# Retention and mLSTM heads issued in turn on TensorE with four branch-gate projections between them, in other buffers and another order on VectorE and ScalarE

## What is computed

```python
hx = modulate(rms_norm(x, norm1_gain[layer]), sh1, sc1)
feats_x, post_x = mixer_inputs(hx, w_in[layer], mlstm_gate_bias[layer], rope)
ret_x, ml_x, _, _ = bidirectional_scans(feats_x, log_gamma[layer], st_f, st_b)
x = x + g1 * mixer_output(ret_x, ml_x, *post_x, w_ret_up[layer], w_ml_up[layer], w_out[layer])
x = x + g2 * swiglu(modulate(rms_norm(x, norm2_gain[layer]), sh2, sc2), w_ffn_in[layer], w_ffn_out[layer])
...
def mixer_output(ret, ml, rg, mo, bg_ret, bg_ml, w_ret_up, w_ml_up, w_out):
    y_ret = from_heads(head_norm(ret)).astype(dtype) * jax.nn.silu(rg)
    y_ml = from_heads(head_norm(jax.nn.sigmoid(to_heads(mo, ML_HEADS)) * ml)).astype(dtype)
    merged = jax.nn.sigmoid(bg_ret) * (y_ret @ w_ret_up) + jax.nn.sigmoid(bg_ml) * (y_ml @ w_ml_up)
    return merged @ w_out
```

## Time and profile before

| | |
|---|---|
| median of 3 runs | 2170.63 us (2169.23 to 2170.95) |
| the profiled execution | 2171.23 us, of it the span from first to last instruction 2169.5 us |
| TensorE busy in the span | 1827.0 us (84%) |
| VectorE, ScalarE, GpSimd busy | 669.6, 325.3, 70.5 us |
| bytes read from HBM | 579.83 MB, 268 GB/s over the span |
| mean granted TensorE clock | 0.915 of full |
| chain that ended last | PE 60%, DMA 32%, DVE 4%, ACT 2% |

### The profile page before, as it was taken

How to read it: one execution, slowest core, us unless ns; L and a number is a source line. 1 busy time by engine, 2 the same in 40 slices (tenths; PEclk the granted TensorE clock), 3 DMA queues, 4 the chain that set the end, 5 groups by cost and what they waited for, 6 DMA issues and landing times.

```text
span 2169.5 us, 23007 instructions
## 1 busy us (share of the span) xinstructions
PE 1827.0 (84%) x9806; PEld 1118.0 (52%) x9806; DVE 669.6 (31%) x1390; ACT 325.3 (15%) x668; POOL 70.5 (3%) x82
## 2 busy tenths in 40 slices
PE   7999789999998999998998888888999755565555
PEld 4557578788886456656443222224577522222222
DVE  3874265187832024523111011113232200000002
ACT  4101230100101123311110000003232100000001
POOL 0001210000000000000000000000040000000000
PEclk8999999999998975797999999999999888878888
DMA  9488225567536110021999999995322599999996
GB/s 410 205 367 330 78 83 228 195 271 286 223 121 255 70 54 1 1 78 64 429 428 427 428 428 428 427 426 217 121 112 78 218 428 427 427 427 427 427 427 260
DMA packets 42150, 582.37 MB, mean 268 GB/s; under 512 B 4672, under 2 KB 4928, under 8 KB 6080
## 3 DMA queue, kind: packets, MB, share of 16 engines
q1 hardware_dynamic: 42048, 580.90, 64.7%
HBM read 579.83 MB, written 1.05 MB: 268 GB/s over the span
## 4 chain that ended last, share of the span: by engine, by line
PE 60%; DMA 32%; DVE 4%; ACT 2%; issue 1%; POOL 1%; SPq 0%; DVEq 0%; ACTq 0%; POOLq 0%
PE banks L622 41%; DMA ring<-in_experts_dram 31%; PE banks L1145 6%; PE banks L1166 3%; PE banks L920 3%; PE banks L531 2%; PE banks L967 1%; PE banks L607 1%; DMA ring<-in_weights_dram 1%; DVE ring L1783 1%; DVE banks L1817 1%; PE banks L582 0%; PE banks L594 0%; PE banks L1233 0%; DVE hT L1855 0%
## 5 line engine op out<-in xcount | busy, mean ns | idle before, releaser
L1145 PE MATMUL banks<-ring,arena 128*32 128x256 f32 (+1 forms) x3072 | 398.6, 524 | 175.2 <-DMA ring<-in_experts_dram 173.4
L622 PE MATMUL banks<-hT,ring 128*128 128x256 f32 (+2 forms) x1776 | 407.4, 391 | 14.1 <-ACT hT L1401 12.2
L622 PEld LDWEIGHTS banks<-hT,ring 128*128 128x128 f32 (+1 forms) x1776 | 336.4, 190 | 84.6 <-issue 40.5
L1145 PEld LDWEIGHTS banks<-ring,arena 128*32 128x32 f32 (+1 forms) x3072 | 145.7, 134 | 426.0 <-DMA ring<-in_experts_dram 243.5
L1783 DVE SCALAR_TENSOR_TENSOR ring<-ring,sil_c 128x512 f32<-128x512 f32 x336 | 242.6, 750 | 7.9
L1166 PE MATMUL banks<-ring,arena 128*32 128x256 f32 (+1 forms) x1536 | 185.8, 486 | 67.0 <-DMA ring<-in_experts_dram 50.9
L2361 DVE TENSOR_TENSOR arena<-arena,banks 128x512 f32<-128x512 f32 (+1 forms) x32 | 17.7, 554 | 543.1 <-PE banks L1145 543.1
L622 PE MATMUL banks<-ring,hT 128*128 128x512 f32 (+1 forms) x448 | 176.1, 553 | 3.3 <-DVE arena L1992 3.3
L622 PE MATMUL banks<-arena,ring 128*128 128x256 f32 (+2 forms) x656 | 170.8, 421 | 2.7 <-POOL arena L2492 1.6
L622 PE MATMUL banks<-arena 128*128 128x64 f32 (+3 forms) x736 | 142.3, 354 | 23.8 <-POOL arena L2486 16.0
L1166 PEld LDWEIGHTS banks<-ring,arena 128*32 128x32 f32 (+1 forms) x1536 | 69.6, 126 | 166.7 <-issue 78.8
(11 more groups left out here) (279 smaller groups left out, 1135.9 us busy)
## 6 DMA issues: line engine op xcount, KB each, us to landing
ring<-in_experts_dram SPq DMA_DIRECT2D x192, 2048.0 KB, 30.5
ring<-in_weights_dram SPq DMA_DIRECT2D x73, 2048.0 KB, 11.5
ring<-in_weights_dram SPq DMA_DIRECT2D x8, 1408.0 KB, 7.3
ring<-in_weights_dram SPq DMA_DIRECT2D x2, 1152.0 KB, 26.5
cT<-in_ctx_dram SPq DMA_DIRECT2D x2, 1024.0 KB, 7.5
ring<-in_weights_dram SPq DMA_DIRECT2D x2, 1024.0 KB, 15.4
ring<-in_weights_dram SPq DMA_DIRECT2D x1, 1536.0 KB, 28.3
xT<-in_x_dram SPq DMA_DIRECT2D x1, 1024.0 KB, 7.1
```

Source lines behind the costliest of these rows:

```text
L622: ins = mm(dst, a, b, start=(i == 0), stop=(i == len(terms) - 1))
L1145: ins = mm(banks[M * q:M * q + M, which, 0:W], xc[:, 4 * half + k, :], w[:, k, W * q:W * q + W], start=(half == 0 and k == 0), stop=(half ...
```

## The change

Six things are changed:

- **TensorE.** The two head loops become one. For each h it issues gate projection h (`bg00`, `bg01`, `bg10`, `bg11`), both kinds of scores of head h+1, then both kinds of values of head h. The gates of b = 2 and 3 follow after the loop.
- **Buffers.** `p_ret` and `q_ret`, which overlapped `p_ml` and `q_ml` in the arena, move into the first half of slot `EARLY`, which holds `mod_acc[0]`. ScalarE and VectorE therefore wait once for `modT3`. `sig_r` moves to `hctx`, `yT` and `merged` move within the arena.
- **ScalarE.** The first four gate jobs are copied raw into `sig_r` between the heads; one Sigmoid over 2048 columns follows after the norms. It copies all four `yT` jobs.
- **VectorE.** The two head loops become one as well. `mod_sum` of c0 and c1 stays behind `y_normed`; c2 moves to just before the first `wo` residual and c3 to between the second and the third. Its two `yT` copies go away.
- **GpSimd.** The multiplications of the two kinds of heads alternate.
- **Order of the weights.** bg0 bg1 bg2 c0 bg3 c1 r_up c2 m_up c3, where it was bg0 c0 bg1 c1 bg2 c2 bg3 c3 r_up m_up.

The core of the diff:

```diff
-    for b in range(4):
-        w8(f"bg{b}", w_in, 4112 + 512 * b, 512)
-        w8(f"c{b}", m_w[1], 512 * b, 512)
+    for n in ("bg0", "bg1", "bg2", "c0", "bg3", "c1"):
...
     w8("r_up", w["w_ret_up"][0], 0, D)
+    w8("c2", m_w[1], 512 * 2, 512)
     w8("m_up", w["w_ml_up"][0], 0, D)
+    w8("c3", m_w[1], 512 * 3, 512)
...
-        p_ret = carve(G0 + 768, 2, 512)
-        q_ret = carve(G0 + 1792, 2, 2, N)
+        p_ret = ring[:, EARLY, 0:1024].rearrange("p (a n) -> p a n", a=2)
+        q_ret = ring[:, EARLY, 1024:2048].rearrange("p (a d n) -> p a d n", a=2, d=2)
...
-        yT = hctx
-        sig_r, sig_m = carve(0, KD, N), carve(2048, KD, N)
-        merged = carve(4096, KD, N)
+        yT = carve(4096, KD, N)
+        sig_r, sig_m = hctx, carve(0, KD, N)
+        merged = carve(6160, KD, N)
...
@@ TensorE @@
+            ret_scores(0)
+            ml_scores(0)
+            for h in range(HEADS):
+                branch_gate(h // 2, h % 2)
                 if h + 1 < HEADS:
+                    ret_scores(h + 1)
                     ml_scores(h + 1)
...
+                ret_values(h)
+                ml_values(h)
+            for b in (2, 3):
                 for a in range(2):
...
+                    branch_gate(b, a)
@@ ScalarE @@
+            def gate_copy(h):
+
+                job = f"bg{h // 2}{h % 2}"
+                eng.wait_ge(*jobs.is_filled(job))
+                A(flat(sig_r[:, 2 * h:2 * h + 2, :]), jobs.bank(job)[:, :], ACT.Copy).then_inc(*act.frees(job))
...
+            ret_decays(0)
+            eng.wait_ge(flag("mc_rep"), 1)
             ml_exps(0)
             for h in range(HEADS):
+                gate_copy(h)
+                if h + 1 < HEADS:
+                    ret_decays(h + 1)
+                    ml_exps(h + 1)
                 ml_abs(h)
...
+            A(flat(sig_r), flat(sig_r), ACT.Sigmoid).then_inc(*act.raises("sig_r"))
+            for b in (2, 3):
...
@@ VectorE @@
+            ret_weights(0)
             ml_weights(0)
             for h in range(HEADS):
+                ml_scored(h)
+                if h + 1 < HEADS:
+                    ret_weights(h + 1)
+                    ml_weights(h + 1)
+                ret_out(h)
                 ml_out(h)
...
-            for b in range(4):
-                mod_sum("c", b)
...
+            mod_sum("c", 0)
+            mod_sum("c", 1)
...
             for a in range(4):
+                if a in (0, 2):
+                    mod_sum("c", 2 + a // 2)
                 residual(f"wo{a}", xT, 2 * a, 0, 2, 0)
```

More of the change, by code:

```diff
@@ L749, in ret_scores, with ret_values @@
                                  for s in range(TC)]).then_inc(*jobs.fills(job))
-            eng.wait_ge(*jobs.is_drained("s_ret1"))
-            ret_scores(0)
-            for h in range(HEADS):
-                if h + 1 < HEADS:
-                    ret_scores(h + 1)
+            def ret_values(h):
                 eng.wait_ge(flag("ret_q"), 2 * h + 2)
@@ L766, in _, with branch_gate @@
                                  for c in range(TC)]).then_inc(*jobs.fills(job))
+            def branch_gate(b, a):
+                eng.wait_ge(*arrives(f"bg{b}"))
+                w = slot(f"bg{b}", 512)
+                job = f"bg{b}{a}"
+                if jobs.new(job) > 1:
+                    eng.wait_ge(*jobs.is_free(job))
+                o = jobs.bank(job)
+                project([(o[:, N * j:N * j + N],
+                                  [(w[:, k, P * (2 * a + j):P * (2 * a + j) + P], hlat[:, k, :])
+                                   for k in range(KD)]) for j in range(2)]).then_inc(*jobs.fills(job))
+                used(f"bg{b}", job)
+            eng.wait_ge(*jobs.is_drained("s_ret1"))
             eng.wait_ge(*jobs.is_drained("s_ml11"))
@@ L784, in ml_scores, with ml_values @@
                                  for s in range(TC)]).then_inc(*jobs.fills(job))
-            ml_scores(0)
-            for h in range(HEADS):
+            def ml_values(h):
                 eng.wait_ge(flag("ml_q"), 2 * h + 2)
@@ L826, in _ @@
             ups = [slot("r_up", D), slot("m_up", D)]
-            eng.wait_ge(*jobs.is_drained("yT01"))
-            eng.wait_ge(*jobs.is_drained("yT11"))
+            for m in range(2):
+                for a in range(2):
+                    eng.wait_ge(*jobs.is_drained(f"yT{m}{a}"))
             for n in range(KD):
@@ L1488, in _, with ret_decays @@
                 A(mo[:, c, :], o[:, :], ACT.Sigmoid).then_inc(*act.frees(f"x_mo{c}"))
-            for h in range(HEADS):
+            def ret_decays(h):
                 if h >= 2:
                     eng.wait_ge(*jobs.is_filled(f"ro{h - 2}"))
+                elif h == 0:
+                    eng.wait_ge(*jobs.is_filled("modT3"))
                 for d in range(2):
@@ L1541, in _ @@
                     o = jobs.bank(f"bg{b}{a}")
-                    dst = (sig_r, sig_m)[b // 2][:, 4 * (b % 2) + 2 * a:4 * (b % 2) + 2 * a + 2, :]
-                    A(flat(dst), o[:, :], ACT.Sigmoid).then_inc(*act.frees(f"bg{b}{a}"))
-            for a in range(2):
-                eng.wait_ge(*jobs.is_filled(f"yT0{a}"))
-                o = jobs.bank(f"yT0{a}")
-                A(flat(yT[:, 2 * a:2 * a + 2, :]), o[:, :], ACT.Copy).then_inc(*act.frees(f"yT0{a}"))
+                    n = 4 * (b % 2) + 2 * a
+                    A(flat(sig_m[:, n:n + 2, :]), o[:, :], ACT.Sigmoid).then_inc(*act.frees(f"bg{b}{a}"))
+            for m in range(2):
+                for a in range(2):
+                    eng.wait_ge(*jobs.is_filled(f"yT{m}{a}"))
+                    o = jobs.bank(f"yT{m}{a}")
+                    A(flat(yT[:, 4 * m + 2 * a:4 * m + 2 * a + 2, :]), o[:, :], ACT.Copy).then_inc(*act.frees(f"yT{m}{a}"))
             squares(0, xT, [[f"wo{a}"] for a in range(4)])
@@ L2034, in _, with ret_weights @@
             eng.wait_ge(flag("decays_whole"), 1)
-            for h in range(HEADS):
+            def ret_weights(h):
                 if h >= 2:
                     eng.wait_ge(*jobs.is_filled(f"ro{h - 2}"))
+                elif h == 0:
+                    eng.wait_ge(*jobs.is_filled("modT3"))
                 eng.wait_ge(*jobs.is_filled(f"rs{h}"))
@@ L2113, in _ @@
                 ins.then_inc(*dve.raises("y_normed"))
-            for b in range(4):
-                mod_sum("c", b)
-            for a in range(2):
-                eng.wait_ge(*jobs.is_filled(f"yT1{a}"))
-                o = jobs.bank(f"yT1{a}")
-                V.tensor_copy(flat(yT[:, 4 + 2 * a:6 + 2 * a, :]), o[:, :]).then_inc(*dve.frees(f"yT1{a}"))
+            mod_sum("c", 0)
+            mod_sum("c", 1)
             eng.wait_ge(*jobs.is_drained("bg31"))
```

26 lines of the change are left out of this document (7 added, 19 removed).

## The result

| | before | changed |
|---|---|---|
| median, run side by side | 2170.2 us (2169.23 to 2170.95, 4 runs) | 2140.85 us (2139.14 to 2143.64, 4 runs) |
| ratio | | 0.9867, 95% interval 0.9852 to 0.9881 |
| the profiled execution | 2171.23 us | 2140.57 us |
| span | 2169.5 us | 2138.8 us |
| mean granted TensorE clock | 0.915 | 0.918 |

A forecast was written before the change was run, and what follows sets the result against it. TensorE was taken to bound everything up to the first expert. From the profiled 2171.23 us, -29.9 (head stage), +0.1 (yT copies) and +0.2 (handovers) gave 2141.6; the median, 0.6 lower, 2141.0 us, range 2138 to 2152.

The forecast's parts named there:

- five terms: Head stage on TensorE at full clock: scores 6.9, retention values 7.3, mLSTM values 9.1, broadcasts 4.5, four gates 27.7 us.
- The two parts of the gain: Head stage: of 29.9 us, 20.7 is idle time, the other 9 matmuls no longer at a clock of 0.80.
- rival 1: Head stage: only the idle time goes, gain 20.7 us, total 2149.9; chance 0.08.
- a cover of 16.6 us: Merged head loop: TensorE work between a head's broadcasts and first mLSTM values, against a chain of 6.4, at most 12.2.
- a matter of latency: Old head stage: waits blamed on the three-engine chain between scores and values, 6.4 us for head 1.
- Predicted reserve: VectorE's sums: c0 and c1 end at 33.1 us, first up result 34.1; c3 leaves 0.9 before the last residual.
- Rival 2: wo stage: VectorE or a weight block sticks out, up to 11.1 us, up to 2152.1; chance 0.04.
- the list of signs of being wrong: Idle before mLSTM values, clock under 0.9, gap before up from ScalarE, VectorE idle before norm squares, gain lost by end.
- The 0.2 us for handovers: Head stage: added cost for one more change between kinds of work per head, 0.2 us.
- Rival 4: Expert stages: time never reaches the end because the experts' weights bind from the start, 2170.6; chance 0.02.
- rival 5: Later attention changes clock: even at full, down to 2088 (0.03), or odd at 0.50, 2176 (0.01); chance 0.04.
- Rival 3: Merged head stage: clock drops and stays at 0.50, 25.6 us slower, 2196.2; chance 0.03.

The follow-up runs named there:

- Experiment 3: Old kernel with seven matmuls whose results are overwritten put before the wait of each mLSTM head; 2165.47 us, ratio 0.9979.
- experiment 1: Changed kernel with all eight gate projections behind the heads, the two kinds of heads still interleaved; 2148.72 us, ratio 0.9906.
- (7): The kernel of experiment 1 with one PSUM bank skipped in each turn of the head loop; 2150.52 us, ratio 0.9909.
- experiment 9: The kernel of experiment 1 with VectorE multiplying the next head's mLSTM scores before the current head's mLSTM outputs; 2145.33 us, ratio 0.9884.
- (4): Changed kernel with the sums of c2 and c3 back behind c0 and c1, ahead of the up products; 2141.72 us, ratio 0.9869.
- (5): Changed kernel with the sum of c3 one residual later, between the third and last wo residual; 2146.15 us, ratio 0.9889.

## Why the prediction was right

**The stage.** 55.5 us were predicted and 55.63 measured, from five terms of which one was off. By the starts in the timeline a gate job takes 6.90 us (27.6 for four, 27.7 predicted), the broadcasts 1.06 (4.2 and 4.5), the retention values 1.79 (7.2 and 7.3) and the mLSTM values 2.23 (8.9 and 9.1). The scores take 0.96 us for 4 records, 7.7 us in all and not 6.9: the price of 0.2165 us a record came from groups of 16 matmuls into one bank, and two matmuls of a job of their own take 0.24 a record, presumably by the step between jobs, which no run isolates. The other terms were a little high and gave it back.

**The two parts of the gain.** 20.7 us of idle time all went, and the clock rose from 0.85 to 1.00. Experiment 3 shows 7.7 us of the second part by itself, on the old order. That refutes rival 1, by which only the idle time would go. The prediction put the whole 9 us down to the clock, though, and 1.3 of them are something else. In the retention part of the old kernel the clock was 1.00 already:

```profile
238.20:254.60 16.40, 11.66 (x81) 9.98 (x79) 4.04 (x7) 5.94 (x10) 5.59 (x8) 1.00 0.36 129
```

But a group behind a wait takes some 0.16 us more up to the next start even where the clock is 1.00: 1.95 us for 16 records of retention values (252.66 to 254.61) against 1.79, 2.40 for the mLSTM values of experiment 3 (267.14 to 269.54) against 2.23. Eight waits make 1.3 us.

**The chain.** Head 1's weighted scores were ready on VectorE at 257.4 us and their values began at 265.60, 8.2 us of reserve. The prediction had put a cover of 16.6 us against 12.2 at most, that is 4.4 or more. The chain itself took 9.5 us (from the broadcasts at 247.88) and not 6.4, since the outputs of head 0 stand before it on VectorE; that was inside its bound. But the prediction had called the old waits a matter of latency, "not any engine's rate", from 23.27 us of VectorE work in 58: in experiments 1, 7 and 9, with the gates out between the heads, every wait of TensorE in the heads ends with VectorE's weighted scores or 0.10 us after them (L2105 of experiment 9 ends at 269.73, the values start at 269.83, though their bracket names GpSimd), and by the timelines VectorE's turn for one pair (8.2 us, where it had counted 5.8 of work) sets the pace of TensorE. Busy time left out some 1.4 us of pauses between dependent steps and 1.0 of waiting for ScalarE. With a turn of 13.9 us this did no harm.

**The sums.** Predicted reserve 1.0 us before the first `up` product and 0.9 before the last residual; measured 1.25 and 1.01. Rival 2, a sum that sticks out, has its price now: 3.3 us with all sums ahead, 6.35 with the last one late, and not 11.1, since only the part past the cover is paid, but with 1.7 and some 2.7 us of low clock on top of it.

**Where a detail was wrong at no cost.** The Sigmoid did not fit before the fifth gate was filled. That was at 299.6 us, and it ran from 303.35 to 305.26, because the norm's squares and root and two table loads of 1.28 us stand ahead of it. The fifth gate's bank was read at 305.17, 5.6 us late, and nobody needed it yet. The four copies of `yT` on ScalarE cost nothing: `up` waits for 1.09 us, and 1.15 before, where 0.1 had been added. A gap before `up` that ends with ScalarE stood in the list of signs of being wrong; it is there, but it only replaces one of the same length that ended with VectorE, so the sign was badly chosen. The weights were in time: no wait of TensorE between 237 and 400 us ends with a DMA.

**The end.** The 0.2 us for handovers and the 0.1 for the copies were not there to be seen; 29.6 was predicted for the whole and 29.5 measured from the first scores to the end. Rival 4 (it never reaches the end) is refuted by that, rival 5 (a later stage changes its clock) by the windows of the attention, 0.50 and 1.00 as before. Rival 3, the slow one, is refuted by the clock of 1.00 over the stage, and not only thanks to the gates: in experiment 1 the matmuls of the heads stood alone, and the clock was 1.00 too. Why the even attention stays at 0.50 no run tested. That the median of 2140.85 lies 0.15 us from the 2141.0 is partly luck, as the 1.17 us of earlier start were in no term; two further sets of runs of the same kernel gave 2138.66 and 2138.84. The other buffers and the new order of the weights are in every run on the changed kernel, so no run says what they are worth by themselves.

## What to carry to other kernels

Price a reordered stage as the sum of its matmuls at full clock, and look at the mean time of the rows behind each wait too: 20.7 us of waits here were worth 29.7, most of the rest because the matmuls behind them ran at the low clock. To ask whether a chain hides, don't compare another engine's busy time with the cover but the length of its list for one turn, pauses and waits for third engines included: VectorE had 5.8 us of work in a turn that took 8.2. And when work fills a gap, look for what is next: two waits of 1.1 and 1.65 us were left, and taking them away gave 3.25 us more (2135.91 us against 2138.84 for the changed kernel beside it).

## What the runs showed besides

**Some waits are paid again behind their end.** From the timelines: behind waits of 1.09 and 1.65 us, and ones of 2.28 and 2.39, the matmuls took about their usual time (27.89 us for `wo` behind 1.65; 2.02 and 2.05 against 1.95 for retention values behind 2.28 and 2.39). Behind 2.41 they took 3.95 against 2.40 (experiment 9), behind 3.25 they took 3.58 against 1.95 (7), behind 3.29 they took 29.58 against 27.89 (4): 1.6 to 1.7 us each time. Behind 4.06 it was some 2.7 us over two groups (5), and behind the four waits of 3.33 to 4.58 us in the old kernel's mLSTM part 1.7 to 2.3 each. The length of the wait alone doesn't settle it: near 32 us of the changed kernel, where short waits follow each other closely, 16 records of L549 took 3.20 us behind a wait of 1.44, and 1.92 just before. So the wait before `wo` that grew by 1.64 us cost 3.3.

**The start moves from one execution to another.** The first scores began at 238.20 us in the old kernel and between 232.95 and 240.10 in the others; 235.54, 236.72 and 237.03 are all of the changed kernel. The difference is there by 90 us: a group of 48 records of 512 columns starts at 86.77 us in the old kernel, at 87.30 in the changed one, at 83.21 in experiment 1 and at 88.77 in experiment 9. Behind a wait of 3.25 us the old kernel took 22.56 us for this group, where the changed one took 20.87 behind one of 1.78: 1.69 us again. Three executions of one kernel lay 1.5 us apart; whether the other 5 us belong to the kernels or to their executions was not settled. It is why medians that differ by less than some 4 us say little here, and why the stretches were counted from the first scores.
